# Experts stage: the first tile in two halves of its slots, early rows in places that hold no weights, its chain first on TensorE

## The reference, cut to what matters

```python
x = x + mod[2] * (y @ w_out[l])
h2 = modulate(x, norm2_g[l], mod[3], mod[4])
x = x + mod[5] * peer_ffn(h2, peer_wq[l], peer_subkeys[l], peer_u[l], peer_v[l])
...
# peer_ffn, per block of tokens: 8 heads, 2 x 128 sub-keys, top 16 of each head
v1, i1 = lax.top_k(s1, 16); v2, i2 = lax.top_k(s2, 16)
top, pos = lax.top_k(cand, 16)
eid = jnp.take_along_axis(cid, pos, axis=-1)          # 8 x 16 = 128 experts per token
gate = jax.nn.softmax(top, axis=-1)
act = jax.nn.gelu(jnp.einsum('td,thkd->thk', hx, u[eid]))
return jnp.einsum('thk,thkd->td', gate * act, v[eid])
```

## Time and profile before

| | |
|---|---|
| median of three runs | 4,569.44 us |
| the profiled execution | its span, 4,564.8 us, is what is known of its time |
| TensorE, VectorE, ScalarE, POOL busy | 2,219.0, 2,602.0, 447.4, 2,589.7 us |
| gathers | 2,560, in 368,640 packets, 1,342.34 MB, 74.2% of the 16 DMA engines' span |
| first gather of layer 0, of layer 1 | 756.20, 3,203.57 us from the span's start |

### The profile page before, as it was taken

The page is one execution under the profiler, slowest core; times in us unless marked ns, Lnnn a source line. Parts: engine busy times, 40 slices in busy tenths (PEclk is TensorE's granted clock), DMA queues, the critical chain, the costliest instruction groups (busy, mean ns, idle before and its releaser), DMA issues. The chain is left out here.

```text
span 4564.8 us, 35548 instructions
## 1 busy us (share of the span) xinstructions
PE 2219.0 (49%) x11745; PEld 1075.9 (24%) x11745; DVE 2602.0 (57%) x5865; ACT 447.4 (10%) x936; POOL 2589.7 (57%) x2779
## 2 busy tenths in 40 slices
PE   7996889343053052051165787698415025025034
PEld 2434665110010010010023644365401001001001
DVE  2116568963954945946845700456983873872940
ACT  1004541000000000000000000352100000000000
POOL 1103302777767767777767563220677767767765
PEclk9997899777576576576567898789758558558568
DMA  6840033999999999999999998102899999999998
GB/s 223 278 160 30 22 109 137 396 409 409 410 409 409 409 400 409 410 401 409 409 393 407 400 403 342 69 21 100 324 409 409 410 409 408 410 404 403 410 408 333
DMA packets 453076, 1497.28 MB, mean 328 GB/s; under 512 B 60786, under 2 KB 94150, under 8 KB 446110
## 3 DMA queue, kind: packets, MB, share of 16 engines
q0 software_dynamic: 368640, 1342.34, 74.2%
q1 hardware_dynamic: 46808, 82.78, 5.3%
q10 hardware_dynamic: 37446, 69.88, 4.6%
HBM read 1477.10 MB, written 17.73 MB: 327 GB/s over the span
## 5 line engine op out<-in xcount | busy, mean ns | idle before, releaser
L1757 POOL DMA_INDIRECT experts_U<-in_peer_u_dram,experts_expert x768 | 727.4, 947 | 713.4 <-PE experts_acc L1986 442.2
L2317 DVE CUSTOM_DVE_ANT_0 experts_U<-experts_U,experts_acc 128x1024 f32<-128x1024 f32 x768 | 929.0, 1219 | 62.2 <-DMA experts_U<-in_peer_u_dram,experts_expert 35.1
L2317 DVE CUSTOM_DVE_ANT_0 experts_V<-experts_V,experts_acc 128x1024 f32<-128x1024 f32 x512 | 621.0, 1220 | 580.9 <-DMA experts_V<-in_peer_u_dram,experts_expert 562.2
L1764 POOL DMA_INDIRECT experts_V<-in_peer_v_dram,experts_turned x640 | 605.4, 946 | 273.0 <-issue 176.2
L1764 POOL DMA_INDIRECT experts_U<-in_peer_v_dram,experts_turned x640 | 608.4, 951 | 234.0 <-issue 164.1
L2133 PE MATMUL experts_pair<-small,experts_w 128*128 128x128 f32 x10 | 4.7, 475 | 1383.8 <-DVE experts_w L2276 1383.8
L2147 PE MATMUL experts_acc<-experts_U,experts_lent 128*32 128x512 f32 x2560 | 436.8, 814 | 351.1 <-DMA experts_U<-in_peer_v_dram,experts_turned 351.1
L2147 PE MATMUL experts_acc<-experts_V,experts_lent 128*32 128x512 f32 x2560 | 428.6, 800 | 325.2 <-DMA experts_V<-in_peer_v_dram,experts_turned 325.2
L1757 POOL DMA_INDIRECT experts_V<-in_peer_u_dram,experts_expert x512 | 484.9, 947 | 174.4 <-issue 104.4
L2133 PEld LDWEIGHTS experts_pair<-small,experts_w 128*128 128x128 f32 x10 | 1.8, 183 | 1386.4 <-DVE experts_w L2276 1386.4
L428 PE MATMUL proj_acc<-W,HT 128*128 128x512 f32 (+3 forms) x752 | 295.8, 547 | 17.5 <-DMA W<-in_w_in_dram 15.2
(11 more groups left out here) (273 smaller groups left out, 3080.0 us busy)
## 6 DMA issues: line engine op xcount, KB each, us to landing
proj_ada<-in_ada_w_dram ACTq DMA_DIRECT2D x40, 1024.0 KB, 5.5
W<-in_w_in_dram SPq DMA_DIRECT2D x9, 2048.0 KB, 12.8
experts_U<-in_peer_u_dram,experts_expert POOLq DMA_INDIRECT x768, 14.0
experts_QT<-in_w_in_dram ACTq DMA_DIRECT2D x12, 960.0 KB, 18.4
experts_V<-in_peer_v_dram,experts_turned POOLq DMA_INDIRECT x640, 12.9
experts_U<-in_peer_v_dram,experts_turned POOLq DMA_INDIRECT x640, 12.8
PR<-in_ada_w_dram SPq DMA_DIRECT2D x8, 1024.0 KB, 17.4
experts_U<-in_w_out_dram SPq DMA_DIRECT2D x4, 2048.0 KB, 11.8
```

Source lines behind the costliest of these rows:

```text
L1757: pool.indirect_dma_start(into, None, u_rows, bass.IndirectOffsetOnAxis(ap=s.expert[:, j % 2, k:k + 1], axis=0)).then_inc(done, 16)
L1764: pool.indirect_dma_start(into, None, v_rows, bass.IndirectOffsetOnAxis(ap=s.turned[:, j % 2, e:e + 1], axis=0)).then_inc(done, 16)
L2317: nc.vector.tensor_tensor_reduce(out=rows, in0=rows, in1=h_bank(), scale=1.0, scalar=0.0, op0=ALU.mult, op1=ALU.add, accum_out=s.dots[:, j ...
```

## The change

- The first tile becomes two segments of 64 slots (`segs`): U of the first half, V of the first half, U of the second half, V of the second half. A V gather of a half brings the 64 slots of two tokens, so a half has 64 of them, in 16 groups.
- The first tile's first 64 U gathers use the six places of `lent`, which is free once h of tile 0 is no longer read there; the next 128 gathers use `lent` and the two halves of `turn_out`, eight places; from the second half's V rows on the ring has 16 places (`lent`, `turn_out` and `s.V`). `s.U` is no ring any more: it holds `w_out`, then the transposed h of the other tiles, the spread weights and a pair tile of zeros.
- TensorE runs tile 0's transposes, queries and scores ahead of tile 1's second half projection; the projections of tiles 2 and on follow, each half released by a residual. VectorE searches and chooses the first four heads straight behind tile 1's first residual, then runs the first 64 dots with one residual behind every sixth (`RESIDUALS_AT`). The first 32 dots read h from SBUF, since the PSUM banks still serve transposes. The second half's search, and the normalisation of tiles 2 and on, follow the first half's weights.
- The wide queries move behind the first half's weighted sums and use one PSUM bank; the last key scores stand before group 3, the late transposes before groups 10 to 13. SP loads the context stream's three rows after `wq`.

```diff
-    TURNED_AT = [76] + [48] * (T - 1)
+    HALF = SLOTS // 2
+    segs = [(0, 0, HALF), (0, HALF, HALF)] + [(j, 0, SLOTS) for j in range(1, T)]
+    TURNED_AT = [28, 48] + [48] * (T - 1)
+    FROM_BANK = 32
+    LENT = NT
+    HALF_STEP_AT = [0, 2, 4, 6]
+    LAST_SCORES_AT = 3
+    LATE_AT = [10, 11, 12, 13]
+    RESIDUALS_AT = 6
...
+        for n in range(2 * dots_to[-1]):
+            if n < HALF:
+                p = n % LENT
+            elif n < v_number(1, 0):
+                p = (n - HALF) % RING
+            else:
+                p = (n - v_number(1, 0) + RING) % PLACES
...
             def _(pool):
-                pool.wait_ge(prods, 2 * T)
                 def wait_free(n):
+                    was = before[n]
+                    if was is None:
+                        if n == LENT - 1:
+                            pool.wait_ge(qprods, 2)
+                        elif n == HALF + LENT:
+                            pool.wait_ge(prods, 2 * T)
+                        elif n == v_number(1, 0):
                             pool.wait_ge(qprods, QUERIES)
                         return
+                    if k < segs[q][2]:
+                        pool.wait_ge(dots, dots_to[q] + k + 1)
+                    elif (k - segs[q][2]) % GROUP == 0:
+                        pool.wait_ge(sums, groups_to[q] + (k - segs[q][2]) // GROUP + 1)
...
                 def wide_queries(h):
-                    pe.wait_ge(qev, 3 + h)
+                    if h == 0:
+                        pe.wait_ge(late_ev, 2 * (T - 1))
+                    pe.wait_ge(qev, 4 + h)
...
                 transposes("y", 2)
                 project_out(1, 0)
-                project_out(1, 1)
                 transposes("h", 0)
                 queries(0, (0,))
-                transposes("y", 3)
                 pe.wait_ge(subbed, 1)
                 scores(0, 0)
-                project_out(2, 0)
+                project_out(1, 1)
                 scores(0, 1)
                 queries(0, (1,))
+                transposes("y", 3)
+                project_out(2, 0)
+                scores(0, 2)
                 project_out(2, 1)
...
+                    if i == 3:
+                        turn_experts(0)
                     project_out(i, 1)
...
+                normalise(0)
+                evacuate("h", 0)
                 residual(1, 0)
+                for _ in retrieve_half(nc, dve, link, s, sems, ps, l, 0):
+                    pass
                 residual(1, 1)
...
+                def beside_dots(k):
+                    if k == 0 and n_s == 2:
+                        dve.wait_ge(coef_in2, 16)
+                        coefficients(0)
+                    if k == 2:
+                        average(1)
+                    if k == 4:
+                        normalise(1)
+                    n, off = divmod(k, RESIDUALS_AT)
+                    if off == 0 and 1 <= n <= 2 * (T - 2):
+                        if n == 1 and n_s == 2:
+                            dve.wait_ge(gate_in, 32)
+                        residual(2 + (n - 1) // 2, (n - 1) % 2)
...
-                        nc.vector.tensor_tensor_reduce(out=rows, in0=rows, in1=h_bank(),
+                        nc.vector.tensor_tensor_reduce(out=rows, in0=rows, in1=s.H[:, tiles[0]] if q == 0 and k < FROM_BANK else h_bank(),
...
                     weigh(q)
+                    if q == 0:
+                        rest_of_head()
```

More of the change, by code:

```diff
@@ L1509, in split_places, with choose @@
     link.hold(at)
-def choose(nc, link, s, sems, l, place, first):
+def choose(nc, link, s, sems, l, place, first, paired=False):
     HH = PH // 2
@@ L1559, in retrieve, with retrieve_half, softmax_exp @@
         yield from choose(nc, link, s, sems, l, place, first)
[L1560 to L1576, removed]
+    yield from soften(nc, dve, link, s, sems, j + 1, place)
+def retrieve_half(nc, dve, link, s, sems, ps, l, first):
+    for h in range(first, first + PH // 2):
+        yield from search(nc, dve, link, s, sems, ps, h)
+    yield from split_places(nc, link, s, first, PH // 2)
+    yield from choose(nc, link, s, sems, l, 0, first, paired=True)
+    shift_scores(nc, s, sems, first, PH // 2)
+def softmax_exp(nc, act, s, sems, n, first=0, count=PH):
+    heads = slice(first * TOPK, (first + count) * TOPK)
+    act.wait_ge(sems.shifted, n + 1)
+    nc.scalar.activation(s.soft[:, heads], s.soft[:, heads], ACT.Exp).then_inc(sems.soft, 1)
 def search_sems(st):
@@ L1699, in query_banks @@
         def query_banks(i):
[L1700 to L1711, removed]
@@ L1729, in experts @@
+        def place_of(n):
+            p = home[n]
+            return near(p) if p < RING else s.V[:, p - RING], ug[p] if p < RING else vg[p - RING], 16 * turn_of[n]
         with nc.Block() as block:
@@ L2198, in normalise, with coefficients @@
                     nc.vector.tensor_tensor(Y[:, t], Y[:, t], sh[:, x], ALU.add).then_inc(hs, 1)
-                finding = retrieve_by_halves(nc, dve, link, s, sems, ps, l)
-                def pieces(n):
-                    for _ in range(n):
-                        next(finding, None)
+                def coefficients(x):
+                    link(nc.vector.scalar_tensor_tensor(out=sc[:, x], in0=sc[:, x], scalar=1.0, in1=g, op0=ALU.add, op1=ALU.mult))
                 nc.vector.tensor_scalar(rstat[:, 1, 0:n_heads], rstat[:, 0, 0:n_heads], 1.0 / 128, EPS, ALU.mult, ALU.add).then_inc(means, 1)
@@ L2218, in _ @@
                 nc.vector.tensor_copy(s.sub[:], ps[:, 0, 0:NKEYS]).then_inc(subbed, 1)
-                dve.wait_ge(coef_in, 16 * (1 + n_s))
-                for x in range(n_s):
-                    link(nc.vector.scalar_tensor_tensor(out=sc[:, x], in0=sc[:, x], scalar=1.0, in1=g, op0=ALU.add, op1=ALU.mult))
-                dve.wait_ge(gate_in, 32)
-                dve.wait_ge(shift_in, 16 * n_s)
+                for i in range(4, T):
+                    norm_heads(i)
+                dve.wait_ge(coef_in, 32)
+                coefficients(n_s - 1)
+                dve.wait_ge(gate_in, 16)
+                dve.wait_ge(shift_in, 16)
                 residual(0, 0)
```

434 lines of the change are left out of this document (234 added, 200 removed).

## The result

The changed kernel takes **4,587.95 us** (median; 4,578.69 to 4,591.32), the kernel before, run beside it, 4,569.4. The ratio is 1.0042, 95% interval 1.003 to 1.0055: slower by 18.5 us, where the prediction had 16 and a range from 4,558 to 4,645. The profiled execution took 4,588.88 us, its span 4,587.1 against 4,564.8.

What follows compares the result with a forecast made beforehand. It took DMA bandwidth, near 409 GB/s while gathering, as the bound. Up to the 193rd gather layer 0 changes by -2 and layer 1 by +18; +16 on the 4,569.4 us median gives 4,585 us, range 4,558 to 4,645.

Steps and rivals of the forecast that it cites:

- Earlier start: First half's ids wait for one shorter chain, so the first gather comes 44.0 us earlier in layer 0, 13.9 in layer 1.
- First gather to the 64th dot: First 64 U gathers in six places, rounds of 7.8 to 8.5 us: 99 us in layer 0, 96 in layer 1.
- The landing of 6.3: Time a gather takes to land, taken as 6.3 us, with 5.1 and 8.0 as ends; one more microsecond costs 33.
- held issues: First 32 dots read h from SBUF and hold the gather issued beside them: 0.74 us added to each round of six.
- V stretch: First half's V gathers in eight places freed by fours: a new wait, rounds of 14.0 us, 110.6 us per layer.
- Second half's U: Next 64 U gathers in eight places at the DMA's 1.28 us each: 82 us.
- Its cover: Eight wide queries through one bank, 64 us in layer 0, fit under 77 us of U gathers: cover 13 us.
- Sum: Change up to the 193rd gather, start included: -2 us in layer 0, +18 in layer 1, together +16.
- Rival 1: Gathers land in 5.1 us because queues are emptier: layers -15 and +2, 4,557 us; chance 0.17.
- The estimate of 3.2: Skill's gather landing, 2.0 us plus bytes at 436 GB/s; end near 4,522 us, left as tail of Rival 1.
- Rival 2: Gathers land in 8.0 us, as at layer 0's start: layers +29 and +51, 4,649 us; chance 0.21.
- Rival 3: TensorE, idling at the lower clock, becomes the pace: a half projection 14.0 us against 8.2, 4,673 us; chance 0.07.

Runs made afterwards that it cites:

- e3_chain_later: Changed kernel with tile 1's second half projection put back ahead of tile 0's transposes, queries and scores on TensorE; 4,594.66 us.
- e1_v12: Changed kernel with 12 places instead of 8 for the first half's V gathers; 4,527.03 us, 0.9914 of the kernel before.
- e8_bank_alone: Changed kernel with h read from PSUM from the 24th dot in layer 0 and the 4th in layer 1, instead of the 32nd; 4,575.94 us.
- e2_bank64: Changed kernel with all 64 dots of the first half reading h from SBUF, not only the first 32; 4,591.12 us.
- e4_u4: Changed kernel with four places instead of six for the first half's U gathers; 4,623.54 us.
- e5_u7: e1_v12 with a seventh place for the first 64 U gathers; 4,522.04 us, 0.9899 of the kernel before.

## Why the prediction was right

Measured against its steps (prediction in brackets), layer 0 / layer 1, from the two profiles:

- **Earlier start**: counted from the third tile's transposes (663.51 and 3,140.97 in the earlier trace rows) 92.7 and 62.6 us before, 48.0 in both layers after: 44.6 / 14.6 (44.0 / 13.9). Each link of the chain had a row, and e3_chain_later shows one link at its price.
- **First gather to the 64th dot**: 106.9 / 99.4 (99 / 96); over the three kernels with this part alike 104.3 / 100.4. This is the term that was undersized, by 4 to 5. The landing of 6.3 was right (6.1 by e1_v12's row). Of the held issues the prediction took 0.74 per round, 3.9 for 32 dots; e8_bank_alone and e2_bank64 give 11.3 us for 60 dots of layer 1, 6.0 for 32. It did look at the right row, but a round has six gathers and up to three of them were held. By parts, at the mean of the three kernels: the first dot ends 5.6 and 5.5 us after the first gather, where the sum has 7.5; the next 31 dots take 52.8 and 52.1, where it has 47.9 and 46.7; the last 32 take 46.0 and 42.8, where it has 43.8 and 41.7. Most of the miss lies beside the dots from SBUF, and a shorter first landing hid 2 us of it. The mechanism differs there too: between the 6th and the 38th gather of the changed kernel POOL's issue of 1.29 and 1.22 us, with 0.30 ahead of it, fills 95% of the 1.67 and 1.60 per gather. The pace was POOL's issue and not, as priced, the places' round with one hold in it. Why the last 32 take longer than priced isn't told apart.
- **V stretch**: 107.1 / 109.4 (110.6). Round 14.1 and 13.9 (14.0), landing 6.33, 6.12 and 6.56 (6.3), sums 3.68 in layer 1 (3.6), 296 to 301 GB/s (300). That this wait costs its 110 - 82 us was shown by taking it away, in e1_v12.
- **Second half's U**: 84.4 / 82.6 (82). Its cover held: the wide queries took 57.1 us and 4.7 of gaps, 61.8 (64), and the next 80 us run at 409 GB/s.
- **Sum**: 298.4 - 250.3 - 44.6 = +3.5 (-2) and 291.3 - 256.8 - 14.6 = +19.9 (+18), together +23.4 (+16). Behind the 193rd gathers layer 0 gains 1.7 and layer 1 2.6 back; the stages ahead of the two layers took 1.1 and 2.1 longer. That is the 22.3 by which the spans differ; the medians differ by 18.5. That the forecast's 16 came so near to 18.5 is partly luck: up to the 193rd gathers the sum was 7.4 short, though layer 0's V stretch was priced 3.5 too high, and the medians lie 3.8 nearer to each other than the spans.

Rival 1 (landing 5.1) fails by the landing rows, 6.1 at the median with six places and 6.12 to 6.56 in the V rounds behind the first (5.66); its own condition, emptier queues, does shorten them, but as e4_u4 shows only to 5.4 with four. The estimate of 3.2 by the Trainium skill (DMA: Bandwidth & Descriptors, Anatomy of one DMA — SWDGE (gpsimd) path) isn't borne out by any of these rows. Rival 2 (8.0) fails by the same rows. Rival 3, TensorE at the lower clock as the pace, isn't seen: the clock granted in layer 0's first part was 0.85 and 0.80, and VectorE's idle time there is put down to transfers, none to a projection, as its groups in 712 to 820 show:

```profile
L2396 DVE CUSTOM_DVE_ANT_0 experts_lent<-experts_lent,Y 128x1024 f32<-128x1024 f32 x32 | 38.3, 1224 | 9.0 <-DMA experts_lent<-in_peer_u_dram,experts_expert 8.9
L2396 DVE CUSTOM_DVE_ANT_0 experts_lent<-experts_lent,experts_acc 128x1024 f32<-128x1024 f32 x32 | 38.0, 1216 | 5.9 <-DMA experts_lent<-in_peer_u_dram,experts_expert 5.6
...
L2243 DVE TENSOR_TENSOR experts_half<-experts_acc,experts_G 128x512 f32<-128x512 f32 x9 | 6.2, 684 | 0.0
```

## What to carry to other kernels

An earlier start is worth only what the stretch behind it keeps: price a ring of places as places over (release + issues + landing + consumer), and where places come free by groups, count groups in flight; here two groups of four left the DMA at 300 GB/s of 409, and three brought it to 390. Before giving a start away again, look for memory that is idle for just that stretch, here two gate rows, the half-output tile and one tile of the weights' memory. When a bound has been lifted, compute the next one from all engines, the issuing one with its holds included, before expecting the whole gain.

## What was not expected of the hardware

An issue beside back-to-back dots with both inputs in SBUF took up to 1.99 us, over twice the 0.94 beside dots from PSUM, where the kernel before had shown 1.68 beside a single such instruction. And the landing of the same 512 KB went with the number in flight: 5.4 us with four places, 6.1 with six, both for U rows, and 7.7 in another stretch, the V rows of e1_v12 with twelve, whose row of the DMA view is

```profile
experts_lent<-in_peer_v_dram,experts_turned POOLq DMA_INDIRECT x34, 7.7
```

So taking a place away cost less here than a fixed landing would give (e4_u4). That adding one brings less for this reason is an inference: in e5_u7, where a seventh was added, POOL's issue already set the pace.
